# Neighbourhood attention in a fused fp32 model: scores of an even and an odd head issued as a pair, and keys stored without zero rows

## What is computed

```python
# 8 rows x 64 columns of tokens; NA_KH, NA_KW = 8, 16; 8 heads of 64
def neighbourhood_mixer(q, k, v, rpb):
    ...
    key_cols = cs[:, None] + jnp.arange(NA_KW)[None, :]
    ...
    s = jnp.einsum('bchd,bcnhd->bhcn', q_row, kg, preferred_element_type=jnp.float32) * scale
    s = s + bias.astype(jnp.float32)[None]
    p = jax.nn.softmax(s, axis=-1).astype(v.dtype)
    return jnp.einsum('bhcn,bcnhd->bchd', p, vg)
```

## Time and profile before

| | |
|---|---|
| time before, median of 3 runs | 2614.06 us (2610.14 to 2617.79) |
| profiled execution, its own time | 2617.82 us |
| profiled execution, span | 2616.0 us |
| PE busy | 2505.3 us, 96% |
| POOL busy | 1933.5 us, 74% |
| DVE busy | 1112.2 us, 43% |
| ACT busy | 683.9 us, 26% |
| this attention in the first layer, after the last key unit | about 372.5 to 411.7 us of the span |

### The profile page before, as it was taken

How to read it: one execution, slowest core, us unless ns; L and a number is a source line. 1 busy time by engine, 2 the same in 40 slices (tenths; PEclk the granted TensorE clock), 3 DMA queues, 4 the chain that set the end, 5 groups by cost and what they waited for, 6 DMA issues and landing times.

```text
span 2616.0 us, 37880 instructions
## 1 busy us (share of the span) xinstructions
PE 2505.3 (96%) x12926; PEld 2004.2 (77%) x12926; DVE 1112.2 (43%) x1618; ACT 683.9 (26%) x1299; POOL 1933.5 (74%) x1567
## 2 busy tenths in 40 slices
PE   7999999999999999999999999999999999979997
PEld 6776777777788887777687777788887777758776
DVE  4556443234222224636625223422225338650775
ACT  3445233112201012526315111210002215231341
POOL 6777855989889888867873899998988573447704
PEclk9999999999999999999999999999999899979998
DMA  3232421223233322322421323333333121112201
GB/s 133 89 97 97 154 73 53 86 92 98 90 98 96 97 94 81 96 81 92 167 89 35 93 88 98 90 97 96 98 96 97 57 81 58 41 35 89 73 26 64
DMA packets 67568, 226.60 MB, mean 87 GB/s; under 512 B 7552, under 2 KB 16256, under 8 KB 66944
## 3 DMA queue, kind: packets, MB, share of 16 engines
q1 hardware_dynamic: 66736, 223.95, 27.0%
q10 hardware_dynamic: 720, 1.17, 0.1%
HBM read 222.99 MB, written 2.10 MB: 86 GB/s over the span
## 4 chain that ended last, share of the span: by engine, by line
POOL 36%; PE 32%; issue 21%; DVE 6%; DMA 4%; POOLq 2%; ACT 1%; SPq 0%; DVEq 0%; ACTq 0%
POOL whi L473 17%; POOL wlo L476 12%; PE ps L569 8%; PE ps L570 8%; PE ps L571 8%; POOL raw L492 3%; POOL ada_acc L494 3%; DMA raw<-w_gate 2%; DMA raw<-w_abc 1%; PE ps L678 1%; PE ps L647 1%; PE ps L603 1%; DVE q_parts L1853 1%; POOLq L475 1%; DMA raw<-w 1%
## 5 line engine op out<-in xcount | busy, mean ns | idle before, releaser
L473 POOL TENSOR_TENSOR whi<-raw,one 128x512 fp32r<-128x512 f32 (+3 forms) x732 | 794.0, 1085 | 551.3 <-PE ps L571 474.1
L476 POOL TENSOR_TENSOR wlo<-raw,whi 128x512 fp32r<-128x512 f32 (+3 forms) x732 | 951.4, 1300 | 57.3
L569 PE MATMUL ps<-h,whi 128*128 128x512 f32 x1984 | 797.4, 402 | 38.8 <-POOL wlo L476 20.2
L570 PE MATMUL ps<-h,whi 128*128 128x512 f32 x1984 | 781.9, 394 | 0.0
L571 PE MATMUL ps<-h,wlo 128*128 128x512 f32 x1984 | 781.2, 394 | 0.0
L569 PEld LDWEIGHTS ps<-h,whi 128*128 128x128 f32 x1984 | 377.3, 190 | 141.2 <-POOL wlo L476 33.3
L571 PEld LDWEIGHTS ps<-h,wlo 128*128 128x128 f32 x1984 | 377.0, 190 | 82.2
L570 PEld LDWEIGHTS ps<-h,whi 128*128 128x128 f32 x1984 | 378.0, 191 | 79.0 <-issue 2.4
L569 PE MATMUL ps<-y,whi 128*128 128x512 f32 x640 | 250.9, 392 | 0.6 <-DVE y L1775 0.6
L570 PE MATMUL ps<-y,whi 128*128 128x512 f32 x640 | 249.0, 389 | 0.0
L571 PE MATMUL ps<-y,wlo 128*128 128x512 f32 x640 | 249.0, 389 | 0.0
(11 more groups left out here) (283 smaller groups left out, 2960.9 us busy)
## 6 DMA issues: line engine op xcount, KB each, us to landing
raw<-w SPq DMA_DIRECT2D x120, 512.0 KB, 3.5
raw<-w_abc SPq DMA_DIRECT2D x68, 512.0 KB, 3.5
raw<-w_ada SPq DMA_DIRECT2D x48, 512.0 KB, 3.5
raw<-w_gate SPq DMA_DIRECT2D x48, 512.0 KB, 3.5
raw<-w_in SPq DMA_DIRECT2D x44, 512.0 KB, 3.5
raw<-w_pac SPq DMA_DIRECT2D x16, 512.0 KB, 3.5
raw<-w_o SPq DMA_DIRECT2D x16, 512.0 KB, 3.5
raw<-w_out SPq DMA_DIRECT2D x16, 512.0 KB, 3.6
```

What stands on the lines that cost most here:

```text
L473: pool.tensor_tensor(whi[:, s, r], raw[:, s, r], one[:, 0:1].to_broadcast([P, cols // 2]), ALU.mult).then_inc(hi_made, 1)
L476: pool.tensor_tensor(wlo[:, s, r], raw[:, s, r], whi[:, s, r].bitcast(F32), ALU.subtract).then_inc(made, 1)
L569: nc.tensor.matmul(out, whi[:, s, w], moving[:, c, :], start=(c == 0), stop=False)
L570: nc.tensor.matmul(out, whi[:, s, w], rest[:, c, :], start=False, stop=False)
```

## The change

- `kc` becomes 4 tiles instead of 8: both heads of a tile in place, no zero rows. The two memsets and the semaphore `kc_zeroed` go. `c_keys` writes a whole tile of 128 rows with one operation instead of two of 64 rows.
- A score matmul contracts over the 64 rows of its head only: rows 0 to 63 for an even head, rows 64 to 127 for an odd one.
- With `paired=True` PE issues no score in an even step; in an odd step i it issues `score(i + 3)` (even head) and `score(i + 4)` (odd head) one after the other. The lists of DVE and ACT stay as they are, and so does the place of `values`.
- The wait for the key tile of heads 4 and 5 moves from before `score(4)` to the end of `c_qk_rest`, ahead of `turn(0)`.

```diff
-        kc_ = at("kc", [P, C_HEADS, T], hd + 4 * TILE)
+        kc_ = at("kc", [P, C_TILES, T], hd + 4 * TILE)
...
                     if i < n:
                         turn(i)
-                        if i + ahead < n:
+                        if paired:
+                            for k in (i + ahead - 1, i + ahead):
+                                if i % 2 == 1 and k < n:
+                                    score(k)
+                        elif i + ahead < n:
                             score(i + ahead)
                     if i >= 2 and i % 2 == 0:
                         values(i - 2)
...
                     for s in (1, 0, 1):
                         unit(s, DC, h_hi, h_lo)
+                    pe.wait_ge(bank_free[0], free_n[0].now() + 1)
...
-                pe.wait_ge(kc_zeroed, kz_n.next())
...
-                    if b == 0 and hh in (4, 6):
+                    if (b, hh) == (0, 6):
                         pe.wait_ge(bank_free[hh // 2 - 2], free_n[hh // 2 - 2].now() + 1)
-                    return nc.tensor.matmul(ps[bank][:, 0:C_WIN], qc_[:, hh // 2, b * P:(b + 1) * P],
-                                            kc_[:, hh, C_START[b]:C_START[b] + C_WIN], start=True, stop=True)
+                    r = slice(HD * (hh % 2), HD * (hh % 2) + HD)
+                    return nc.tensor.matmul(ps[bank][:, 0:C_WIN], qc_[r, hh // 2, b * P:(b + 1) * P],
+                                            kc_[r, hh // 2, C_START[b]:C_START[b] + C_WIN], start=True, stop=True)
...
-                          between=c_qk_rest, ready=v_read)
+                          between=c_qk_rest, ready=v_read, paired=True)
...
-                nc.vector.memset(kc_[HD:P, 0::2, :], 0.0)
-                nc.vector.memset(kc_[0:HD, 1::2, :], 0.0).then_inc(kc_zeroed, 1)
...
-                        for half in range(2):
-                            r = slice(HD * half, HD * half + HD)
-                            to, frm = by_column(kc_[r, 2 * (first + t) + half, :], ps[t][r, :])
-                            _, by = by_column(kc_[r, 2 * (first + t) + half, :], rsb[r, :])
-                            last = nc.vector.tensor_tensor(to, frm, by, ALU.mult)
-                        last.then_inc(bank_free[t], 1)
+                        to, frm = by_column(kc_[:, first + t, :], ps[t][:])
+                        _, by = by_column(kc_[:, first + t, :], rsb[:])
+                        nc.vector.tensor_tensor(to, frm, by, ALU.mult).then_inc(bank_free[t], 1)
```

More of the change, by code:

```diff
@@ L295, in build @@
         bias_in = sem("bias_in")
-        kc_zeroed = sem("kc_zeroed")
         sig_ready = sem("sig_ready")
@@ L552, in _ @@
             p_n, pt_n, on_n, y_n, nm_n, mod_n = Count(), Count(), Count(), Count(), Count(), Count()
-            pr_n, mg_n, kv_n, bs_n, kz_n, rb_n = Count(), Count(), Count(), Count(), Count(), Count()
+            pr_n, mg_n, kv_n, bs_n, rb_n = Count(), Count(), Count(), Count(), Count()
             qn_n, qs_n, chu_n, dft_n, fou_n, y2_n, ex_n = Count(), Count(), Count(), Count(), Count(), Count(), Count()
@@ L624, in attention @@
             def attention(n_heads, scores, value, chunks, ring, slots, banks, o_banks, r_bank, o_read=None, between=None,
-                          ready=None):
+                          ready=None, paired=False):
                 n = NQB * n_heads
@@ L703, in _ @@
                                     (nope_n, 4),
-                                    (p_n, 80), (pt_n, 80), (on_n, 12), (y_n, 12), (nm_n, 80), (mod_n, 1), (kv_n, KV_STEPS), (bs_n, 2), (kz_n, 1), (rb_n, 3), (rd_n, 12),
+                                    (p_n, 80), (pt_n, 80), (on_n, 12), (y_n, 12), (nm_n, 80), (mod_n, 1), (kv_n, KV_STEPS), (bs_n, 2), (rb_n, 3), (rd_n, 12),
                                     (pr_n, 3 * DC), (mg_n, DC + FF_TILES)]):
```

## The result

| | before | after |
|---|---|---|
| median, measured side by side | 2615.93 us (2610.14 to 2620.45) | 2641.3 us (2639.29 to 2649.35) |
| ratio, 95% interval | | 1.0102 [1.0085, 1.0118] |
| span of the profiled execution | 2616.0 | 2639.0 |
| the stage, layer 1 | 39.01 | 48.94 |
| the stage, layer 2 | 39.01 | 52.51 |

The kernel is 1.0% slower. I forecast slower, but 2626 us, and 2641.3 lies outside my range of 2612 to 2634. It grew by 9.93 us in layer 1 and by 13.50 in layer 2, 23.4 in all, and the spans differ by 23.0. That the rest agrees to 0.4 us is chance: in the traces of all runs it lies between 2531 and 2545 us.

What follows compares the result with a forecast made beforehand. In the attention ring DVE and PE were held equally near the bound; 9.2 + 5.6 - 2 x 1.1 - 2 x 0.3 = 12.0 us on 2617.8 gave 2629.8, less 3.8 for the median: 2626, range 2612 to 2634.

Steps and rivals of the forecast that it cites:

- block end: Steps 8, 16, 24: even score now behind the reciprocal's wait, +1.5 us three times a layer, 9.2 us in all.
- rhythm: Even scores issued three steps ahead, not four, exposing a chain of waits: about 5.6 us in both layers, bounds 0 and 15.
- keys: Last key operations before the first maximum: one of 128 rows replaces two of 64, gain 1.1 us per layer at most.
- first four scores: Between two units of the PE-bound projection: 1.73 us becomes 1.4, gain 0.3 per layer, bounds 0.8 and -0.3.
- Less lookahead: The forecast's heading for the rhythm: an even score issued three steps after its probabilities' place was turned, formerly four.
- the overlap: Two heads' half-row scores on PE: 0.43 us if fully overlapped, 0.86 if not, taken as 0.65 plus 0.25 for switches.
- memsets: Two of 1.77 us per layer, some 40 us before the stage: removing them gains 0.
- Only the block end counts: Rival: rhythm stays hidden and keys win, 6.4 us, 2620.5; chance 0.24 together with a partly hidden block end (2616).
- PE gains and the ring follows: Rival: fully overlapped heads make PE's pair 1.71 us and the ring ends faster, 14.4 us gained, 2600; chance 0.08.
- No overlap: Rival: 64-row scores run one after the other or switches are dearer, PE's pair 2.34 us, about +16, 2630; chance 0.2.

Runs made afterwards that it cites:

- experiment 5: Kernel after, with the even score of i + 4 issued ahead of the values again in steps 8, 16 and 24 only; 2630.16 us (1.0058).
- Experiment 9: Kernel after with lookahead 6 instead of 4, the values left in their place; 2641.44 us (1.008).
- experiment 4: Kernel after with an even step's values moved behind the next odd step's turn and pair, plus a fourth place for transposed probabilities; 2616.77 us (0.9985).
- experiment 11: experiment 5 with ACT making both copies of a pair of heads, then both exponentials; 2624.87 us (1.0027).
- experiment 2: Kernel before with only the score order changed to pairs in odd steps, keeping full rows and padded keys; 2637.95 us (1.0063).

## Why the prediction was right in direction and short in size

The terms of the sum, as forecast and as the runs show them:

| | forecast | measured | from |
|---|---|---|---|
| block end | 9.2 | 8.5 | 6 x (13.28 - 11.87), experiment 5 |
| rhythm | 5.6 | 13.7 | below |
| keys | -2.2 | -2.3 | first maximum 2.43 behind `turn(0)` before, 1.27 after |
| first four scores | -0.6 | -0.9 | 1.54 to 1.07 between two units |
| clock | none | 3.6 | 52.51 - 48.94 |
| sum | 12.0 | 22.6 | the spans: 23.0 |

**Block end: right.** The hole is 2.62, the maximum of i + 4 begins 2.81 behind the reciprocal (forecast 2.7), the product 3.67 (3.55), the maximum of i + 5 4.26 (4.15). Undoing that one position gives 1.41 per block, where I had 1.53.

**Rhythm: this step failed, in its size.** I had written: "in a block of 8 the output's difference (0.96) fills one half of the 1.9. I take 0.8". The chain was right: from the maximum of an odd step (391.88) to that of the even step three later (395.46) 3.58 us pass, forecast about 3.5. What was wrong is that the difference fills anything. It stands in the chain: it delays the maximum at 391.88, this delays the exponential, this ACT's next copy, the values, the turn and the pair. And it wasn't the only instance. Per block the rhythm costs 2.27 us (11.87 - 9.60), most of it in two holes of 1.0. In the sum: 1.1 before the first reciprocal, which is where the keys' gain went (the first reciprocal comes 9.54 us behind `turn(0)`, before 9.59); 2.27 and 2.17 for the next two distances (9.60 and 9.70 before); and 1.30 for the third (9.58 against 6.87, less the 1.41): 6.86 per layer, 13.7 in both. Against the forecast's 1.0, 0.8, 0.8 and nothing, the first was right, the two whole blocks were almost three times as dear, and the last block was put at nothing because its end is "in any case a chain of the same waits": it cost 1.30 all the same. The forecast's own upper bound for this step was 15; it was held unlikely and left out of the range.

With the rhythm at 13.7 the sum would have been 20 us and the time 2634, at the edge of the range. The rest is the clock's 3.6 us, and 4.3 us by which the medians and spans differ (the kernel before came out at 2615.93 where I had 2614.06, and the medians are 25.4 apart, the spans 23.0), less 0.7 by which the block end was cheaper. Without the clock's part 2641.3 would still lie outside the range.

**A wait that I had not seen.** The values of a block's first two heads wait for the product of the block before, since there is one output bank. In the old order the product was done in time; now it begins 1.6 us later, PE waits 1.34 for it, and the maximum after it has its hole of 0.99. With the block end undone that hole is still 1.01, but then it is PE's own work: PE works without a stop from its spread, which begins 0.25 behind the reciprocal as before, until that pair, which stands behind one more turn and the next values (3.78 us from the spread to the pair; before, that even score came 2.39 behind the spread).

**"Less lookahead" was the wrong name.** Experiment 9 gives two steps more of it and changes nothing; experiment 4 leaves the lookahead and takes all back. What counts is which waits stand in front of a score in PE's list. That the move of the values helps is shown; how the 2.27 divides between ACT's copies and PE's own work stays open, as experiment 11 traded one hole for another.

**Half rows: the overlap was undersized.** Both halves run in full at once. The timeline of PE, kernel after, asked for the scores that begin before 386.20 and then for those before 386.50, shows both first records, one for each head, at once, and both second ones 0.32 later (0.70 less the 0.38 of a record):

```profile
385.95 0.49 PE L905 MATMUL ps<-kc,qc 64*128 64x256 f32 x2
...
385.95 0.70 PE L905 MATMUL ps<-kc,qc 64*128 64x256 f32 x4
```

Two heads' scores take 0.64 until the next turn, and the turn before them is 0.09 longer than with full rows: 0.73 with both switches, where I took 0.90 and full rows need 0.86. I had set the odd head's first record behind the even one's. The Trainium skill (TensorEngine Tiling (Array Packing), Key Properties) says that tiles work independently and in parallel and that a change of mode drains the engine; the trace agrees with both, starts at most 0.01 apart and 0.33 us for a score that goes in and out alone. Of this gain of PE nothing reached the span, as PE was idle for 14 of the 50 us; in the order of experiment 4 it did (1.81 per pair). What did reach it is a loss: from the turn before a pair to DVE's start on its even score 1.10 us pass with half rows (385.59 to 386.69), and 0.91 with full rows (386.36 to 387.27 in experiment 2). Each of the three holes of a block is 0.19 longer by that, and the reciprocals stand 13.28 us apart instead of 12.71.

**Keys and memsets: right.** One operation of 128 rows takes 1.16 us. The memsets were worth nothing, though less safely than I wrote: they end 40 us before the first key operation (70 before the stage), but right behind them stands DVE's copy of spread sums. The timeline of DVE before:

```profile
301.13 1.76 DVE L1678 MEMSET kc<- 64x2048 f32 x1 [0.46 <-issue]
302.85 0.69 DVE L1462 COPY rsb<-ps 128x512 f32<-128x512 f32 x1
```

It begins 1.09 us behind PE's spread (301.76), and without the memsets again 1.09 behind it (304.91 and 303.82).

**The clock was not in the forecast.** I had argued at a clock of 1.00 in the stage. A step that adds idle time to PE can also take its speed, and did so in layer 2 of the kept trace for 3.6 us; of the other executions no stage is on record. Why layer 1 was spared with the same list stays open.

**The rivals.** "Only the block end counts" fell (2.27 per block beside it). "PE gains and the ring follows" was wrong for this order, for the reason given against it, and in the order of experiment 4 PE does gain (1.81 per pair), but only 0.6 us per stage of it, the keys included, arrives against the kernel before. "No overlap" fell by the trace.

Not tried: the deep lookahead together with four places in PSUM for the transposes (there are two), and a second output bank for the first values of a block.

## What to carry to other kernels

When an instruction is moved in an in-order list, don't count only its own delay: list every wait that now stands ahead of it, and ask for each whether the engine that ends that wait is itself waiting for the moved instruction. A piece of work fills a hole only if it is not itself in the chain that makes the hole. If such a ring closes, change the place of the waiting instruction and not the depth of the buffers; here one move was worth 1.2% (1.0102 to 0.9985) and two more places of lookahead nothing.

## What the runs showed of the hardware that I had not expected

- fp32 scores of two heads in the two halves of the rows start at most 0.01 us apart and cost as much as one (0.70 us from the first start to the last end, for 4 records or for 2). The first record behind a full-array matmul is 0.48 long, the later ones 0.376: going in costs some 0.10, apart from the 0.09 in front. Unpaired they make the block of 8 heads 1.8 us longer (11.40 against 9.60).
- The granted clock fell to the lower level after single waits of PE of at most 1.6 us: in layer 2 of the kernel after, behind three reciprocals of each layer with the product first, in the last 5 us of the stage with the block end undone, behind 1.04 and 0.44 in both kernels with 6 places, and at the end of layer 1 with the other waits filled. The same waits left it at 1.00 in layer 1 of the kernel after. One fall cost 1.2 to 2.0 us of a stage.
